# The seven level products of a gated head: taken in three groups over four banks, instead of one by one over two

## The chip, the cores and the metric

One core of one Trainium2 chip runs the whole program. The metric is the time on the device in microseconds (us), lower is better. A core has five engines that run their own instruction streams and wait for each other by semaphores: TensorE (PE in the rows, PEld for its weight loads), VectorE (DVE), ScalarE (ACT), GpSimd (POOL) and SyncE (SP), which issues the transfers.

## The reference

Two transformer blocks of two layers each, on 512 tokens of width 1024, in float32. The change touches one mixer of the second block, a gated linear recurrence over eight heads of key and value width 128:

```python
S_t = diag(f_t) S_{t-1} + k_t v_t^T ;  o_t = S_t^T q_t
scores = einsum('bhtk,bhsk,bhtsk->bhts', qc, kc, decay)   # decay = exp(b_t - b_s), b = cumsum(log f), s <= t
...
o = rmsnorm(o, norm_gain) * sigmoid(g) ;  return o @ w_o
```

The decay differs by key channel, so it can't be taken out of the product as one factor.

## The kernel before

**Levels.** Inside each block of 128 tokens the kernel halves the block again and again: `HALVES = [64, 32, 16, 8, 4, 2, 1]`. At level `lv`, each node of 2h tokens is cut into a left and a right half of h tokens, and its middle row of `b_` is the reference point. VectorE writes the differences to the middle into an operand buffer (`sub`), ScalarE takes the exponential of all 512 columns, VectorE multiplies the right halves by the queries and the left halves by the keys (`mul`), TensorE takes four products of 128 x 128 by 128 x 64, one for each token block, and VectorE puts the entries of that level into `hdiag` under a mask (`pred`, a copy_predicated). The diagonal itself comes first, from plain products of keys and queries. What lies between the four blocks comes from four wider products, the cross products, whose operands are `hx128` and `hx256` and whose results leave the banks `tp[0]` and `tp[1]` to `hoff` by ScalarE.

**Buffers.** The three operand buffers `hx[0]`, `hx[1]`, `hx[2]` are named cosT, sinT and negc in the rows; `hx128` and `hx256` are the two halves of wf_raw. Level `lv` uses `hx[lv % 3]` and the bank `sc[lv % 2]`. hdiag_t is `hdiag`, hoff_t is `hoff`.

**Slots.** Each engine's order is written out by hand. `hg_head` runs over 16 slots `k`; an engine does in slot `k` what its branches for that `k` say, in the order in which they stand in the source. In the same slots the projections of the following head are computed ("current" is the head whose scores are made, "following" the next): TensorE has 96 matmuls of 128 x 512 for it (four weight columns, eight k tiles, three terms of a split into a high and a low part), and `share` issues six in each slot, behind the slot's own products. They are the acc rows of line L633. VectorE takes the projected rows out of `acc`, prepares the next head's keys, queries and decays, and splits weights (L1168); ScalarE has the exponentials and logarithms for it.

**Order in a head.** Before, VectorE does `sub(k - 1)`, `mul(k - 2)` and `pred(k - 3)` in slot k; TensorE takes level `lv` in slot `lv + 3`; so each level's result is fetched in the slot in which its product is issued. In slot 9 VectorE normalises the head before (L1692, L1695), in slot 10 it multiplies the cross operands (L1640, L1641), and TensorE takes the cross products in slot 12 (L1054 to L1057). In slot 15 TensorE multiplies `hdiag` and `hoff` by the values (L1066, L1069), once ScalarE has copied `hoff` (L2038, L2039). TensorE runs the slot 0 products of L1035. L2007 is the exponential of a level, L1596 and L1597 are `sub`, L1602 and L1603 `mul`, L1609 `pred`, L633 the projections.

**The last head.** Head 7 has no following head; its slots share only 30 matmuls of the output projection.

Of the kernel before, what the change touches and what calls it, by code (L numbers as in the profile page):

```python
# [25 lines left out]
ACT = mybir.ActivationFunctionType  # L26
# [3 lines left out]
P = 128  # L30
# [81 lines left out]
HG_SLOTS = 16  # L112
HALVES = [64, 32, 16, 8, 4, 2, 1]


# [53 lines left out]
def two_blocks(nc, x, positions, attn_pre_g, w_in, forget_bias, lam_q1, lam_k1, lam_q2, lam_k2, diff_sub_g,  # L169
# [3 lines left out]
    with ExitStack() as ctx:  # L173
# [123 lines left out]
        aux = psum("aux")  # L297
        x_banks = [tp, sc]


# [320 lines left out]
        def _(pe):  # L621
# [395 lines left out]
            def hg_head(pp, par, current=True, following=True, previous=True, first=False, work=()):  # L1017
# [8 lines left out]
                for k in range(HG_SLOTS):  # L1026
                    if current and k == 0:
# [8 lines left out]
                        mm.then_inc(level_scored, 1)  # L1036
                    if current and 3 <= k < 3 + len(HALVES):
                        lv = k - 3
                        h = HALVES[lv]
                        x = hx[lv % 3]  # L1040
                        pe.wait_ge(level_mul, 7 * i + lv + 1)
                        if lv or not first:
                            pe.wait_ge(level_taken, 8 * i + lv)
                        for b in range(NB):
                            right = x[:, b * P:b * P + P].rearrange("p (n e j) -> p n e j", e=2, j=h)[:, :, 1]
                            mm = pe.matmul(sc[lv % 2][:, b * HD:b * HD + HD], x[:, b * P:b * P + P], right,  # L1046
                                           start=True, stop=True)
                        mm.then_inc(level_scored, 1)
                    if current and k == 12:

                        pe.wait_ge(cross_mul, i + 1)
                        if not first:
                            pe.wait_ge(cross_taken, i)
# [54 lines left out]
        def _(v):  # L1108
# [471 lines left out]
            def hg_head(pp, par, current=True, following=True, previous=True, first=False):  # L1580
# [6 lines left out]
                def sub(lv):  # L1587

                    x, b = nodes(hx[lv % 3], HALVES[lv]), nodes(b_, HALVES[lv])
                    h = HALVES[lv]  # L1590
                    mid = b[:, :, 0, h - 1:h].broadcast_to([P, S // (2 * h), h])
                    if lv == 0:
                        v.wait_ge(hg_decay_ready, i + 1)
                    if lv >= 3 or not first:
                        v.wait_ge(level_scored, 8 * i + 1 + lv - 2)
                    TT(x[:, :, 1], b[:, :, 1], mid, ALU.subtract)  # L1596
                    TT(x[:, :, 0], mid, b[:, :, 0], ALU.subtract).then_inc(level_sub, 1)  # L1597

                def mul(lv):
                    x = nodes(hx[lv % 3], HALVES[lv])  # L1600
                    v.wait_ge(level_exp, 7 * i + lv + 1)
                    TT(x[:, :, 1], x[:, :, 1], nodes(q, HALVES[lv])[:, :, 1], ALU.mult)  # L1602
                    TT(x[:, :, 0], x[:, :, 0], nodes(kk, HALVES[lv])[:, :, 0], ALU.mult).then_inc(level_mul, 1)  # L1603

                def pred(lv):
# [4 lines left out]
                                      level_mask[:, lv].rearrange("p (n j) -> p n j", j=HALVES[lv]),  # L1610
                                      sc[lv % 2][:, 0:NB * HD].rearrange("p (n j) -> p n j", j=HALVES[lv])).then_inc(level_taken, 1)

                for k in range(HG_SLOTS):
                    if current:
# [12 lines left out]
                        if 2 <= k < 9:  # L1627
                            mul(k - 2)
                        if 3 <= k < 10:
                            pred(k - 3)  # L1630
                        if k == 7:
# [86 lines left out]
        def _(a):  # L1718
# [275 lines left out]
            def hg_head(pp, par, current=True, following=True, previous=True, first=False):  # L1994
# [4 lines left out]
                for k in range(HG_SLOTS):  # L1999
                    if current:  # L2000
# [3 lines left out]
                        if 1 <= k < 8:  # L2004
                            lv = k - 1
                            a.wait_ge(level_sub, 7 * i + lv + 1)
                            ACTV(hx[lv % 3], hx[lv % 3], ACT.Exp).then_inc(level_exp, 1)  # L2007
                        if k == 11:
# [7 lines left out]
                        if k == 9:  # L2016
                            a.wait_ge(hg_decay_ready, i + 1)
                            a.wait_ge(hg_col_ready, i + 1)
                            if not first:
                                a.wait_ge(cross_scored, i)  # L2020
# [107 lines left out]
```

## Time and profile before

| | |
|---|---|
| time before, median of 3 runs | 2715.2 us (2714.83 to 2715.46) |
| the profiled execution's own time | 2711.78 us |
| its span, first to last instruction | 2710.0 us |
| TensorE busy | 2610.4 us, 96% of the span |
| VectorE busy | 1657.0 us, 61% |
| ScalarE busy | 746.8 us, 28% |
| mean granted TensorE clock | 0.984 |

The gated heads stand at about 2030 to 2308 us of the span. The chain that ended last is 81% TensorE over the whole span. A matmul's recorded duration overlaps its neighbours', so what it costs in a stream is read from one start to the next. Idle time in brackets is counted from the modelled end of the instruction before.

### The profile page before, as it was taken

The numbers are of one execution on the slowest core, as the hardware profiler recorded it, in microseconds if no ns is written. First come the engines' busy times: TensorE is split into PE (matmuls) and PEld (weight loads), VectorE is DVE, ScalarE is ACT, GpSimd is POOL, SyncE is SP. The second block draws the span as 40 slices with busy tenths as digits, with TensorE's granted clock in tenths as the row PEclk, the third lists the DMA queues.
The fourth block names the chain that finished last, engine by engine and source line by source line (L and its number), as shares of the span: only waits on it lengthen the run. The fifth ranks groups of instructions, "written<-read, shape, count | busy, mean of one in ns | idle before, by whom it ended". The sixth has DMA issues, their size and how long they took to land.

```text
span 2710.0 us, 38394 instructions
## 1 busy us (share of the span) xinstructions
PE 2610.4 (96%) x12250; PEld 2059.1 (76%) x12250; DVE 1657.0 (61%) x2625; ACT 746.8 (28%) x1391; POOL 453.5 (17%) x454
## 2 busy tenths in 40 slices
PE   8999899999899989999899989999999999999999
PEld 5776688887667668888766658888888887788887
DVE  6755666454775566645567776644458888564452
ACT  3333232120333332212145541100025555210000
POOL 4111112112111111121201101211111110111111
PEclk9999999999899999999999989999999999999999
DMA  3221233333122123333311113333332221233333
GB/s 110 55 63 54 77 88 100 93 101 101 48 55 63 55 70 101 94 99 94 92 47 55 54 32 94 100 93 101 93 93 63 63 62 47 78 93 100 94 100 94
DMA packets 417270, 214.80 MB, mean 79 GB/s; under 512 B 6819, under 2 KB 416014, under 8 KB 417166
## 3 DMA queue, kind: packets, MB, share of 16 engines
q1 hardware_dynamic: 416144, 212.89, 27.3%
q8 instruction: 59, 0.97, 0.2%
q10 hardware_dynamic: 1022, 0.58, 0.1%
q14 instruction: 45, 0.37, 0.0%
HBM read 211.34 MB, written 2.10 MB: 79 GB/s over the span
## 4 chain that ended last, share of the span: by engine, by line
PE 81%; DVE 10%; ACT 4%; issue 4%; POOL 1%; DVEq 0%; ACTq 0%; POOLq 0%
PE acc L633 69%; PE sc L740 2%; PE sc L1046 1%; DVE scratch L1438 1%; PE tp L633 1%; DVE w_lo L1168 1%; PE tp L763 1%; PE po L786 1%; PE po L633 1%; PE aux L646 1%; DVE scratch L1432 1%; ACT scratch L1914 1%; DVE xT L1357 1%; ACT scratch L1912 0%; PE tp L902 0%
## 5 line engine op out<-in xcount | busy, mean ns | idle before, releaser
L633 PE MATMUL acc<-h_hi,w_hi 128*128 128x512 f32 x1968 | 814.1, 414 | 31.0 <-DVE h_lo L1146 24.2
L576 POOL TENSOR_SCALAR w_hi<-w_raw 128x1024 fp32r<-128x1024 f32 x390 | 415.1, 1065 | 2211.6 <-PE acc L633 2134.3
L633 PE MATMUL acc<-h_hi,w_lo 128*128 128x512 f32 x1968 | 776.0, 394 | 0.0
L633 PE MATMUL acc<-h_lo,w_hi 128*128 128x512 f32 x1968 | 774.7, 394 | 0.0
L1168 DVE TENSOR_TENSOR w_lo<-w_raw,w_hi 128x1024 fp32r<-128x1024 f32 x390 | 477.4, 1224 | 75.6 <-POOL w_hi L576 75.5
L633 PEld LDWEIGHTS acc<-h_hi,w_hi 128*128 128x128 f32 x1968 | 373.2, 190 | 147.3 <-issue 46.4
L633 PE MATMUL acc<-mid_hi,w_hi 128*128 128x512 f32 x1120 | 440.4, 393 | 7.3 <-DVE mid_lo L1699 3.2
L633 PE MATMUL acc<-mid_lo,w_hi 128*128 128x512 f32 x1120 | 439.8, 393 | 0.0
L633 PE MATMUL acc<-mid_hi,w_lo 128*128 128x512 f32 x1120 | 438.6, 392 | 0.0
L633 PEld LDWEIGHTS acc<-h_hi,w_lo 128*128 128x128 f32 x1968 | 372.9, 190 | 81.4 <-issue 1.4
L633 PEld LDWEIGHTS acc<-h_lo,w_hi 128*128 128x128 f32 x1968 | 373.8, 190 | 80.0 <-issue 10.9
L633 PEld LDWEIGHTS acc<-mid_hi,w_hi 128*128 128x128 f32 x1120 | 211.3, 189 | 55.9 <-DVE w_lo L1168 4.5
L633 PEld LDWEIGHTS acc<-mid_lo,w_hi 128*128 128x128 f32 x1120 | 211.4, 189 | 44.7 <-issue 2.1
L633 PEld LDWEIGHTS acc<-mid_hi,w_lo 128*128 128x128 f32 x1120 | 211.3, 189 | 44.2 <-issue 0.8
L1511 DVE TENSOR_TENSOR xT<-xT,acc 128x512 f32 (+1 forms) x80 | 55.0, 688 | 201.8 <-PE acc L633 201.8
L1975 ACT ACTIVATE mid_hi<-scratch 128x512 f32 x64 | 40.5, 633 | 471.9 <-DVE scratch L1550 471.9
L1547 DVE TENSOR_TENSOR scratch<-acc,rstd 128x512 f32<-128x512 f32 x64 | 44.2, 691 | 130.6 <-PE acc L633 122.1
L1293 DVE CUSTOM_DVE_ANT_0 scratch<-sc,mask_row 128x128 f32<-128x128 f32 (+3 forms) x128 | 62.3, 487 | 80.3 <-PE sc L740 40.8
L1825 ACT ACTIVATE scratch<-scratch,stat 128x128 f32<-128x128 f32 (+3 forms) x128 | 72.0, 563 | 134.4 <-DVE stat L1293 134.4
L1883 ACT ACTIVATE mid_hi<-scratch 128x512 f32 x44 | 27.8, 632 | 202.9 <-DVE scratch L1398 202.9
L1736 ACT ACTIVATE scratch<-yT 128x512 f32 x32 | 20.2, 632 | 208.7 <-DVE yT L1366 137.3
L1391 DVE TENSOR_TENSOR scratch<-acc,rstd 128x512 f32<-128x512 f32 x42 | 29.0, 691 | 76.4 <-PE acc L633 76.4
(316 smaller groups left out, 2672.9 us busy)
## 6 DMA issues: line engine op xcount, KB each, us to landing
w_raw<-in_mlp_w_dram SPq DMA_DIRECT2D x128, 512.0 KB, 4.1
w_raw<-in_w_in_dram SPq DMA_DIRECT2D x48, 512.0 KB, 3.9
w_raw<-in_w_gate_dram SPq DMA_DIRECT2D x44, 512.0 KB, 3.8
w_raw<-in_w_up_dram SPq DMA_DIRECT2D x44, 512.0 KB, 3.8
w_raw<-in_w_down_dram SPq DMA_DIRECT2D x32, 512.0 KB, 4.2
w_raw<-in_hg_w_in_dram SPq DMA_DIRECT2D x32, 512.0 KB, 4.1
w_raw<-in_sb_w_qkv_dram SPq DMA_DIRECT2D x24, 512.0 KB, 3.8
w_raw<-in_w_out_dram SPq DMA_DIRECT2D x16, 512.0 KB, 4.1
```

The lines of the kernel that those rows point to most:

```text
L576: nc.gpsimd.tensor_scalar(to, w_raw[:, slot], 1.0, 1.0, ALU.mult, ALU.mult).then_inc(w_rounded, 1)
L633: mm = pe.matmul(bank[:], w[:, k], r[:, k], start=(k == 0 and i == 0), stop=(k == k_tiles - 1 and i == 2))
L646: pe.matmul(aux[:], ones[:, 0:P], pair_sum[q % 2], start=(q == 0), stop=last).then_inc(aux_done if last else square_summed, 1)
L740: mm = pe.matmul(sc[m][:, 0:n], qT[p % 2][r, t * P:t * P + P], kT[p % 2][r, 0:n], start=True, stop=(p < NDIFF))
L1168: TT(w_lo[:, slot], w_raw[:, slot], w_hi[:, slot].bitcast(F32), ALU.subtract).then_inc(w_split, 1)
L1293: v.tensor_tensor_reduce(prob[k % 4][:, 0:n], sc[k % 2][:, 0:n], mask_row[:, S - n:S], 1.0, BIG, ALU.add, ALU.min, stat[:, k % 4:k % 4 + 1 ...
L1391: TT(up, banks[1][:], rstd[:], ALU.mult).then_inc(evacuated[1], 1)
L1511: TT(dst, dst, acc[slot][:], ALU.add).then_inc(evacuated[slot], 1)
L1547: TT(gate, acc[i][:], rstd[:], ALU.mult).then_inc(evacuated[i], 1)
L1825: ACTV(prob[k % 4][:, 0:n], prob[k % 4][:, 0:n], ACT.Exp, bias=stat[:, k % 4:k % 4 + 1], scale=-1.0, accum_out=stat[:, 4 + k % 4:5 + k % 4 ...
L1883: ACTV(mid_hi[:, c % 2, ds(j, 1)], hid, ACT.Copy).then_inc(mid_hi_ready, 1)
L1975: ACTV(mid_hi[:, c % 2, ds(2 * m + i, 1)], hid, ACT.Copy).then_inc(mid_hi_ready, 1)
```

## The change

Level products are issued in three groups: levels 0 and 1 in slot 4, levels 2 and 3 in slot 6, levels 4, 5 and 6 in slot 9. The banks of the seven levels are sc[0], sc[1], tp[0], tp[1], sc[0], sc[1], tp[0], and the operand buffers hx[0], hx[1], hx[2], hx128, hx[0], hx[1], hx[2]. The masked copies go to slots 4, 5, 6, 7, 9, 9 and 10. `sub` and `mul` stay in their slots. The waits follow the buffers and banks: some on the cross products of the head before, one of TensorE's cross products on the last masked copy, one of ScalarE's cross exponentials on the level 3 product. No arithmetic is added or removed.

```diff
+LEVELS_AT = {4: (0, 1), 6: (2, 3), 9: (4, 5, 6)}
+PREDICATED_AT = {4: (0,), 5: (1,), 6: (2,), 7: (3,), 9: (4, 5), 10: (6,)}
...
+        level_x = [hx[0], hx[1], hx[2], hx128, hx[0], hx[1], hx[2]]
+        level_bank = [sc[0], sc[1], tp[0], tp[1], sc[0], sc[1], tp[0]]
...
-                    if current and 3 <= k < 3 + len(HALVES):
-                        lv = k - 3
+                    for lv in LEVELS_AT.get(k, ()) if current else ():
                         h = HALVES[lv]
-                        x = hx[lv % 3]
+                        x = level_x[lv]
                         pe.wait_ge(level_mul, 7 * i + lv + 1)
-                        if lv or not first:
-                            pe.wait_ge(level_taken, 8 * i + lv)
+                        if lv == 1:
+                            pe.wait_ge(level_taken, 8 * i + 1)
+                        if lv == 2 and not first:
+                            pe.wait_ge(cross_taken, i)
+                        if lv >= 4:
+                            pe.wait_ge(level_taken, 8 * i + 2 + lv - 4)
...
                         pe.wait_ge(cross_mul, i + 1)
+                        pe.wait_ge(level_taken, 8 * i + 8)
...
-                    if lv >= 3 or not first:
-                        v.wait_ge(level_scored, 8 * i + 1 + lv - 2)
+                    if lv == 3 and not first:
+                        v.wait_ge(cross_scored, i)
+                    if lv >= 4:
+                        v.wait_ge(level_scored, 8 * i + 2 + lv - 4)
...
-                        if 3 <= k < 10:
-                            pred(k - 3)
+                        for lv in PREDICATED_AT.get(k, ()):
+                            pred(lv)
...
                             a.wait_ge(hg_col_ready, i + 1)
+                            a.wait_ge(level_scored, 8 * i + 5)
```

TensorE in a head of the loop, around what were slots 7 to 9. Before, levels 4, 5 and 6 (L1046, operands cosT, sinT, negc by turns) each stand in front of six projection matmuls; this is level 4, six matmuls and level 5:

```order
L1046 MATMUL sc<-sinT 128x64 x4
L633 MATMUL acc<-h_hi,w_hi 128x512
L633 MATMUL acc<-h_lo,w_hi 128x512
L633 MATMUL acc<-h_hi,w_lo 128x512
L633 MATMUL acc<-h_hi,w_hi 128x512
L633 MATMUL acc<-h_lo,w_hi 128x512
L633 MATMUL acc<-h_hi,w_lo 128x512
```

In the change the three levels stand together in slot 9 (the register rows hold the values of the waits):

```order
L1053 MATMUL sc<-cosT 128x64 x4
L1044 REGISTER_ALU
L1050 REGISTER_ALU
L1053 MATMUL sc<-sinT 128x64 x4
L1044 REGISTER_ALU
L1050 REGISTER_ALU
L1053 MATMUL tp<-negc 128x64 x4
```

Level 4's product moved behind twelve projection matmuls that were behind it, level 5's behind six.

VectorE in the second head, slots 7 to 10. Before (L1609 is the masked copy of levels 4, 5 and 6):

```order
L1609 COPY_PREDICATED hdiag_t<-level_mask,sc 128x64x4
L1635 TENSOR_TENSOR hg_col<-yT 128x1
L1602 TENSOR_TENSOR cosT<-cosT,yT 128x256
L1603 TENSOR_TENSOR cosT<-cosT,yT 128x256
L1609 COPY_PREDICATED hdiag_t<-level_mask,sc 128x128x2
L1660 SCALAR_TENSOR_TENSOR scratch<-scratch 128x512
L1662 TENSOR_TENSOR scratch<-scratch 128x512
L1168 TENSOR_TENSOR w_lo<-w_raw,w_hi 128x1024
L1609 COPY_PREDICATED hdiag_t<-level_mask,sc 128x256
L1692 SCALAR_TENSOR_TENSOR scratch<-scratch,gains 128x512
```

And in the change, from the copy of the same level 4 on (L1619 is the masked copy, L1702 what was L1692, L1650 what was L1640):

```order
L1619 COPY_PREDICATED hdiag_t<-level_mask,sc 128x64x4
L1619 COPY_PREDICATED hdiag_t<-level_mask,sc 128x128x2
L1702 SCALAR_TENSOR_TENSOR scratch<-scratch,gains 128x512
L1705 TENSOR_TENSOR scratch<-scratch 128x512
L1675 TENSOR_SCALAR yT<-scratch,lower 128x512
L1619 COPY_PREDICATED hdiag_t<-level_mask,tp 128x256
L1650 TENSOR_TENSOR wf_raw<-wf_raw,yT 128x2x128
```

The copy of level 5 moved from behind the last `mul` to behind the weight split, and the copy of level 6 to right ahead of the cross operands' multiplies.

## Rows read from the trace of the kernel before

**Rows 1.** Busy by windows: us, PE, PEld, DVE, ACT, POOL; then granted clock.

```profile
2106.00:2142.00 36.00, 35.44 (x194) 29.43 (x193) 30.49 (x66) 19.06 (x37) 4.47 (x4) 1.00 0.21 59
...
2286.00:2310.00 24.00, 20.25 (x104) 16.07 (x104) 14.25 (x38) 11.07 (x24) 0.00 (x0) 0.86 0.04 13
```

**Rows 2.** TensorE's waits, 2036 to 2302 us: total, times, longest.

```profile
PE tp L1054 <- DVE wf_raw L1641: 5.7, 7, 2.6
```

**Rows 3.** Timeline of TensorE in head 2: start, us, instruction.

```profile
2112.15 1.00 PE L1046 MATMUL sc<-sinT 128*128 128x64 f32 x8
2112.96 0.48 PE L633 MATMUL acc<-h_hi,w_hi 128*128 128x512 f32 x1
2113.28 0.39 PE L633 MATMUL acc<-h_lo,w_hi 128*128 128x512 f32 x1
...
2118.76 0.40 PE L633 MATMUL acc<-h_hi,w_lo 128*128 128x512 f32 x1
2119.19 1.10 PE L1046 MATMUL sc<-sinT 128*128 128x64 f32 x8
...
2128.64 0.39 PE L633 MATMUL acc<-h_hi,w_lo 128*128 128x512 f32 x1
2129.54 0.49 PE L1054 MATMUL tp<-wf_raw 128*128 128x128 f32 x2 [0.52 <-DVE wf_raw L1641]
...
2134.84 0.39 PE L633 MATMUL acc<-h_hi,w_lo 128*128 128x512 f32 x1
2135.24 1.13 PE L1066 MATMUL po<-hdiag_t,yT 128*128 128x128 f32 x8
```

**Rows 4.** Timeline of VectorE in head 2.

```profile
2110.63 0.42 DVE L1603 TENSOR_TENSOR sinT<-sinT,yT 128x256 f32<-128x256 f32 x1
...
2113.33 0.45 DVE L1609 COPY_PREDICATED hdiag_t<-level_mask,sc 128x256 f32<-128x256 uint8 x1 [0.51 <-PE sc L1046]
...
2122.74 0.73 DVE L1609 COPY_PREDICATED hdiag_t<-level_mask,sc 128x256 f32<-128x256 uint8 x1 [0.95 <-PE sc L1046]
...
2125.77 0.73 DVE L1609 COPY_PREDICATED hdiag_t<-level_mask,sc 128x256 f32<-128x256 uint8 x1
...
2128.73 0.42 DVE L1640 TENSOR_TENSOR wf_raw<-wf_raw,yT 128x256 f32<-128x256 f32 x1
2129.07 0.42 DVE L1641 TENSOR_TENSOR wf_raw<-wf_raw,yT 128x256 f32<-128x256 f32 x1
```

**Rows 5.** Timeline of ScalarE in head 2.

```profile
2111.30 0.62 ACT L2007 ACTIVATE negc<-negc 128x512 f32<-128x512 f32 x1
...
2134.77 0.37 ACT L2039 ACTIVATE hoff_t<-tp 128x256 f32<-128x256 f32 x1
```

**Rows 6.** Timeline of TensorE in head 0.

```profile
2039.06 1.10 PE L1046 MATMUL sc<-cosT 128*128 128x64 f32 x8 [0.61 <-DVE cosT L1603]
...
2064.39 1.13 PE L1066 MATMUL po<-hdiag_t,yT 128*128 128x128 f32 x8 [0.50 <-ACT hoff_t L2039]
```

**Rows 7.** Timeline of VectorE and TensorE in the last head.

```profile
2295.20 0.74 DVE L1609 COPY_PREDICATED hdiag_t<-level_mask,sc 128x256 f32<-128x256 uint8 x1 [0.26 <-PE sc L1046]
...
2296.56 0.74 DVE L1609 COPY_PREDICATED hdiag_t<-level_mask,sc 128x256 f32<-128x256 uint8 x1 [0.62 <-PE sc L1046]
...
2299.94 0.80 PE L1054 MATMUL tp<-wf_raw 128*128 128x128 f32 x2 [2.57 <-DVE wf_raw L1641]
...
2304.37 1.90 PE L1066 MATMUL po<-hdiag_t,yT 128*128 128x128 f32 x8
...
2314.40 0.51 PE L633 MATMUL acc<-mid_hi,w_hi 128*128 128x512 f32 x1 [3.18 <-DVE mid_lo L1699]
```

**Rows 8.** Busy time by windows around the last head's cross products.

```profile
2300.00:2304.00 4.00, 4.00 (x12) 3.30 (x12) 1.18 (x2) 2.11 (x5) 0.00 (x0) 0.50 0.01 2
...
2312.00:2316.00 4.00, 1.60 (x7) 1.34 (x8) 2.56 (x5) 0.63 (x1) 0.43 (x1) 1.00 0.00 0
```

More of the change, by code:

```diff
@@ L1036, in hg_head @@
                         mm.then_inc(level_scored, 1)
-                    if current and 3 <= k < 3 + len(HALVES):
-                        lv = k - 3
+                    for lv in LEVELS_AT.get(k, ()) if current else ():
                         h = HALVES[lv]
-                        x = hx[lv % 3]
+                        x = level_x[lv]
                         pe.wait_ge(level_mul, 7 * i + lv + 1)
-                        if lv or not first:
-                            pe.wait_ge(level_taken, 8 * i + lv)
+                        if lv == 1:
[4 more added lines that the diff above has]
+                            pe.wait_ge(level_taken, 8 * i + 2 + lv - 4)
                         for b in range(NB):
                             right = x[:, b * P:b * P + P].rearrange("p (n e j) -> p n e j", e=2, j=h)[:, :, 1]
-                            mm = pe.matmul(sc[lv % 2][:, b * HD:b * HD + HD], x[:, b * P:b * P + P], right,
+                            mm = pe.matmul(level_bank[lv][:, b * HD:b * HD + HD], x[:, b * P:b * P + P], right,
                                            start=True, stop=True)
@@ L1587, in sub @@
                 def sub(lv):
-                    x, b = nodes(hx[lv % 3], HALVES[lv]), nodes(b_, HALVES[lv])
+                    x, b = nodes(level_x[lv], HALVES[lv]), nodes(b_, HALVES[lv])
                     h = HALVES[lv]
@@ L1599, in mul @@
                 def mul(lv):
-                    x = nodes(hx[lv % 3], HALVES[lv])
+                    x = nodes(level_x[lv], HALVES[lv])
                     v.wait_ge(level_exp, 7 * i + lv + 1)
@@ L1610, in pred @@
                                       level_mask[:, lv].rearrange("p (n j) -> p n j", j=HALVES[lv]),
-                                      sc[lv % 2][:, 0:NB * HD].rearrange("p (n j) -> p n j", j=HALVES[lv])).then_inc(level_taken, 1)
+                                      level_bank[lv][:, 0:NB * HD].rearrange("p (n j) -> p n j", j=HALVES[lv])).then_inc(level_taken, 1)
                 for k in range(HG_SLOTS):
@@ L2006, in hg_head @@
                             a.wait_ge(level_sub, 7 * i + lv + 1)
-                            ACTV(hx[lv % 3], hx[lv % 3], ACT.Exp).then_inc(level_exp, 1)
+                            ACTV(level_x[lv], level_x[lv], ACT.Exp).then_inc(level_exp, 1)
                         if k == 11:
```

## The prediction

> **What bounds the kernel now.** I read first the busy time by windows. In a middle head TensorE is busy 35.44 of 36 us at a full clock, VectorE 30.49, ScalarE 19.06 [rows 1]. So heads 0 to 6 are bound by TensorE, and only small holes in its stream can be won; VectorE has 5.5 us of room in 36. The last head has few projection matmuls to cover its waits: TensorE is busy 20.25 of 24 us at a mean clock of 0.86 [rows 1].
>
> Next, TensorE's waits: seven times it waits before the cross products for VectorE's multiplies, 5.7 us in all [rows 2]. The longest is the last head's 2.57 [rows 7], which leaves 3.1 us in six heads, 0.52 each.
>
> Then the timeline of TensorE in one middle head, head 2, where a hole is read from start to start. Between 2113.28 and 2118.76 stand sixteen projection matmuls and two levels, 5.48 us: with 0.23 for a matmul, a level has 0.90. That leaves three holes [rows 3]:
> - before level 4, 2118.76 to 2119.19 is 0.43, of which 0.23 is the matmul's: **0.20**;
> - before the cross products, 2128.64 to 2129.54 is 0.90: **0.67**. L1641, the last multiply of the cross operands, releases them;
> - before the value products, 2134.84 to 2135.24 is 0.40: **0.17**. ScalarE's copy of hoff ends at 2134.77 + 0.37 = 2135.14 [rows 5], just ahead of the start.
>
> Last, why VectorE is late with L1641. The last half of its second `mul` starts at 2110.63, and such an instruction takes 0.34 from start to start (2128.73 to 2129.07), so VectorE is free at 2110.97. The cross operands are done at 2129.07 + 0.34 = 2129.41. In these 18.44 us it waits twice for a level's products, 0.51 and 0.95. The copies of levels 5 and 6 also run longer, 0.73 each against 0.45 for level 1's [rows 4]; I count 0.2 more for each. About 1.9 us of the 18.44 is not work.
>
> **The change part by part.**
>
> *Work.* Nothing is added: the same products, subtractions, multiplies and masked copies.
>
> *Joining levels on TensorE.* One level is eight pairs of a weight load and a product: 0.90 us, 0.11 a pair. The first matmul behind it takes 2113.28 - 2112.96 = 0.32 instead of 0.23 [rows 3]. If this 0.09 is paid only on the way out of a group, three groups instead of seven save 4 x 0.09 = 0.35 us in a head; if it only shows that the last pair is still running, nothing. The ends are 0 and 0.35. I take 0, since the 0.90 holds the 0.09 already and is an even eight times 0.11.
>
> The Trainium skill, "TensorE: Matmul & The Clock Gate", section "LDWEIGHTS (loading the stationary operand)", prices a load by its columns at 1.2 GHz: an estimate of 107 ns for 128. By that page eight loads are 0.85 us wherever they stand and joining saves nothing; the row's 0.11 agrees.
>
> *TensorE's order.* In the change level 1 starts where it did, at 2112.15, and level 0 right ahead of it, at 2111.25. Level 6 also keeps its place behind as much work as now. Without the 0.20 hole: before, level 4 would start at 2118.99 and level 6 two slots of 0.90 + 6 x 0.23 = 2.28 later, at 2123.55. New, level 6 starts at 2123.55, level 5 at 2122.65, level 4 at 2121.75.
>
> *The level 4 hole.* Now its operands are ready at about 2119.1, just ahead of 2119.19. In the change `mul(4)` is not later and is wanted at 2121.75. **The 0.20 is gone**, with 2.6 us of cover. Level 6's operands are ready now when VectorE falls idle, 2122.74 - 0.95 = 2121.79, and wanted at 2123.55.
>
> *VectorE up to the cross operands.* It is free at 2110.97 as before. `sub(3)` takes 0.67 and ends at 2111.64. `mul(2)` then waits for ScalarE's exponential, which ends at 2111.30 + 0.62 = 2111.92 [rows 5]: a new wait of 0.3 us. Behind it stand level 0's copy and a weight split for projections two slots on. A result can be copied 2113.33 - 2112.15 = 1.18 us after its level's start [rows 3, 4]; level 0's is there at 2112.43, before VectorE comes. The copies of levels 1, 2 and 3 come a slot behind their products or with one level of work between. Level 3's buffer, hx128, was read last by the head before.
>
> The end of the last `mul`, 2121.79 now, becomes 2121.79 - 0.51 - 0.34 (level 4's copy comes later) + 0.3 = 2121.2. Then two operations for the next head's keys and a split: 2125.77 - 2122.74, less the long copy of 0.54, is 2.5 us [rows 4]. VectorE comes to slot 9's copies at 2123.7. Level 4 can be read from 2121.75 + 1.18 = 2122.93, level 5 from 2123.83, when its copy is due at 2124.0; level 6's from 2124.73, and its copy is due behind the normalising, a microsecond later. Since level 5 has only 0.2 to spare I count 0.3 for waiting there. Of the 1.9 us, 0.6 comes back: the cross operands are done 1.3 earlier, at 2128.1.
>
> *The cross products.* TensorE comes to them at 2128.64 + 0.23 - 0.20 = 2128.67. **The 0.67 is gone**, with 0.5 to spare. Their new wait for the last copy costs nothing, as that copy is ahead of the multiplies on VectorE. ScalarE's cross exponentials follow VectorE's slot 8, which is earlier too; their new wait for level 3's product is some slots old by then.
>
> *The value products.* From cross operands to value products the chain runs over VectorE's scan, ScalarE's logarithms behind it and the copies of hoff: 2135.24 - 2129.41 = 5.83 us. TensorE's own work from cross to value products is 5.70 - 0.17 = 5.53 [rows 3]. New, the chain gives 2128.1 + 5.8 = 2133.9, TensorE 2128.67 + 5.53 = 2134.2. **The 0.17 is gone**, by 0.3: the thinnest margin.
>
> Heads 1 to 6: 6 x (0.20 + 0.67 + 0.17) = 6.2 us. The end with joined levels is 8.3.
>
> *Head 0.* Before level 0 stands a bracket of 0.61, before the value products one of 0.50 [rows 6]. In head 2 a bracket of 0.52 was a hole of 0.67 [rows 3], so these are 0.76 and 0.65. The first is covered by six matmuls in the new slot 4, the second goes as above: 1.4 us.
>
> *Head 7.* VectorE is the chain up to the cross operands. It waits 0.26 and 0.62 for levels 5 and 6, with two long copies [rows 7]: 1.3 us. In the change TensorE still starts each level as soon as its own `mul` is done, and behind level 6's `mul` VectorE has two copies and the normalising before it needs the result. **1.3 us**.
>
> *The clock.* After 2.57 us without a matmul the clock is 0.50, TensorE's 1.2 GHz level [rows 7, 8]. From L1054 to L1066 it takes 4.43 us with four matmuls between; head 2's 5.53 with eighteen gives 5.53 - 14 x 0.23 = 2.31 at a full clock [rows 3, 7], a loss of 2.1. L1066 itself is 1.90 against 1.13: 0.8 more. Together 2.9 us. In the change the hole is 1.3 shorter, and I take it that the clock stays up. Against that, a hole of 3.18 us before 2314.40 left the clock at 1.00 [rows 7, 8], so length isn't all that counts, and this hole, which moves by some 12 us, may fall badly instead: from 0 to as much as the 2.9 just priced. I take -1.5.
>
> The Trainium skill, same page, section "Why this matters for your kernels", asks for no idle gap over about 3 us. The trace doesn't bear it out as a limit: 2.57 us brought the clock down and 3.18 did not.
>
> **Sum:** 6.2 + 1.4 + 1.3 + 2.9 - 1.5 = 10.3 us. Against the profiled execution's 2711.8 that is 2701.5; the timed runs lie 3.4 above it, which I take as a constant: **2704.9 us**.
>
> **The rivals.**
> 1. *Holes go, the clock falls as before.* 8.9 us: 2706.3; with the later hole falling too, 2707.8. For it: nothing shows when the clock is judged.
> 2. *The wait moves to slot 9.* Levels 5 and 6 are read behind a group of three. If their copies wait 0.9 more than I count, one level's work, the cross operands are late by 0.4 and the hoff chain by 0.6, so 0.6 of each head's 1.04 stays: 6 x 0.4 + 1.4 + 1.3 = 5.1, and with half of the clock's 2.9 6.5: 2708.7.
> 3. *Nothing in it.* If new waits take all of VectorE's 1.9 us, only the 0.20 and head 0's 0.76 are won: 2 us, 2713.2. It needs 1.3 us of waiting in slots 4 to 10 that I don't see.
> 4. *Slower.* If a level's result can be copied only when its whole group has ended, level 4's copy waits until 2123.55 + 1.18 = 2124.7, 1.0 us behind VectorE's arrival. That alone leaves the cross operands at 2129.1, still not slower; it decides from 1.3 us on. With 2.5 us (the group's result a whole share late), 7 x 1.2 - 2 = 6.4 slower: 2721.6. Against it: every level's last product has its own increment.
> 5. *Joining saves too.* 7 x 0.35 on top: 2702.4, and 2700.9 without the -1.5.
>
> **How the numbers follow.** My forecast 0.38, rival 1 0.20, rival 2 0.17, rival 3 0.07, rival 4 0.05, rival 5 0.13. The range leaves out rivals 4 and 3 and a piece of rival 2 above, and ends at rival 5 below: 2701 to 2711. About 0.2%, 5.4 us, is what a measurement can tell from no change, so faster means under 2709.8. Faster is 0.38 + 0.20 + 0.13 and most of rival 2, 0.10: 0.81. The same 0.14, slower 0.05.
>
> **What the changed profile would show.** TensorE's waits for wf_raw fall from 5.7 us in seven times to one in the last head, under 2 us; no middle head waits before level 4 or before the value products, and each is 1.0 us shorter; VectorE waits at the masked copies at most once a head, briefly, in slot 9; the clock around the last head's cross products is 1.00. I'm wrong if the cross products of middle heads still wait for VectorE, if the value products wait over 0.3 us for hoff, or if a copy in slot 9 waits 0.9 us.

## The result, and the profile after

The changed kernel takes **2721.8 us** (median of ten runs, 2718.4 to 2727.0) against 2714.7 us before (ten runs beside them, 2712.0 to 2715.8): a ratio of 1.0031, with an interval of 1.0023 to 1.0040. It is slower by about 7 us. The prediction, 2704.9 us in a range of 2701 to 2711, is wrong in its sign.

The profiled execution took 2726.96 us (span 2725.2), the slowest of the ten and 15.2 us more than the 2711.78 before; it had the lowest mean granted clock, 0.977 against 0.978 to 0.984. So what follows shows where the loss lies, and shows the clock's part larger than in the median. I measure a head from the first product L1039 (before: L1035) of one to that of the next. The seven heads 0 to 6 took 247.8 us in the profile before and 260.05 us in this one.

Busy time by windows of the changed kernel (the columns of [rows 1]): two middle heads' worth, two microseconds of head 2 behind its cross products, and the last head from its first product to its value products.

```profile
2106.00:2142.00 36.00, 33.90 (x181) 28.82 (x180) 31.13 (x64) 17.80 (x36) 3.78 (x4) 0.95 0.18 50
2142.00:2178.00 36.00, 33.89 (x191) 28.88 (x189) 31.70 (x64) 18.89 (x37) 4.23 (x4) 1.00 0.19 54
...
2133.00:2135.00 2.00, 2.00 (x8) 1.73 (x7) 1.97 (x6) 0.12 (x1) 0.00 (x0) 0.50 0.00 0
...
2293.00:2320.00 27.00, 24.69 (x100) 20.74 (x99) 19.09 (x47) 12.19 (x26) 1.05 (x1) 0.62 0.07 21
```

TensorE is busy 33.9 of 36 us where it was 35.44 [rows 1]: there is more standing, not less. And the granted clock is 0.95 in the first row, where it was 1.00: part of that stretch, the third row, ran at 0.50.

TensorE's waits, from 2030 to 2325 us: total, times, longest.

```profile
PE tp L1062 <- DVE wf_raw L1651: 12.8, 7, 2.1
PE sc L1053 <- DVE cosT L1613: 1.2, 1, 1.2
PE po L1074 <- ACT hoff_t L2050: 0.6, 1, 0.6
```

The wait that was to vanish, that of the cross products for VectorE's multiplies, has grown from 5.7 us in seven times [rows 2] to 12.8; the last head's is 0.57 of it, the six others 1.9 to 2.1 each. The waits before level 4 and before the value products are gone from the middle heads, as forecast.

Timeline of TensorE in two middle heads, head 2 and head 3: the last projection matmul, the cross products (L1062 on) and the value products (L1074).

```profile
2129.93 0.39 PE L637 MATMUL acc<-h_hi,w_lo 128*128 128x512 f32 x1
...
2132.42 0.77 PE L1062 MATMUL tp<-wf_raw 128*128 128x128 f32 x2 [2.10 <-DVE wf_raw L1651]
2132.98 0.64 PE L1063 MATMUL tp<-wf_raw 128*128 128x128 f32 x2
...
2139.53 1.05 PE L1074 MATMUL po<-hdiag_t,yT 128*128 128x128 f32 x8
...
2170.32 0.46 PE L1062 MATMUL tp<-wf_raw 128*128 128x128 f32 x2 [2.11 <-DVE wf_raw L1651]
2170.61 0.39 PE L1063 MATMUL tp<-wf_raw 128*128 128x128 f32 x2
...
2175.82 1.06 PE L1074 MATMUL po<-hdiag_t,yT 128*128 128x128 f32 x8
```

The hole is 2132.42 - 2129.93 - 0.23 = 2.26 us; it was 0.67. Both heads have it. But in head 2 the rows behind it are long (L1063 0.64 us against 0.39): the clock has fallen to its 1.2 GHz level, and from L1062 to L1074 it takes 7.11 us; in head 3 the clock stayed up and it takes 5.50. So a head is 36.29 us long in head 3 and 37.8 to 37.9 in the five others of heads 1 to 6 (35.4 before). The cost has two parts, then: **0.9 us a head at a full clock, the cross products' hole being 1.6 longer and the other holes gone, and 1.6 us wherever the clock falls behind it**. With head 0, which is 0.87 shorter, that is 6 x 0.9 + 5 x 1.6 - 0.9 = 12.5 us, and the rows show 12.2. The other 3 us of this execution's 15 lie in the last head: it takes 26.9 us from its first product to its value products, at a mean clock of 0.62, where it took 23.84 at 0.89 before. Its clock fell ahead of its cross products, 1.3 us behind a stop of 1.2 us before level 0. I can't put this down to the change: among the thirteen profiled executions of this document, one for each kernel, the stretch is shortest, 21.1 us at 1.00, in experiment 1 and longest, 28.35 us at 0.60, in experiment 2, which has the order of before. Every total contains it.

Why are the cross operands late? Timeline of GpSimd and VectorE in head 2 of the changed kernel: the rounding of the weights (L580, L576 before), and beside each the instruction of VectorE that is longer than its kind.

```profile
2113.30 1.04 POOL L580 TENSOR_SCALAR w_hi<-w_raw 128x1024 fp32r<-128x1024 f32 x1 [6.67 <-PE acc L637]
2113.67 0.95 DVE L1612 TENSOR_TENSOR negc<-negc,yT 128x256 f32<-128x256 f32 x1 [0.23 <-ACT negc L2017]
...
2122.38 1.05 POOL L580 TENSOR_SCALAR w_hi<-w_raw 128x1024 fp32r<-128x1024 f32 x1 [8.04 <-PE acc L637]
2122.41 1.02 DVE L1645 TENSOR_TENSOR hg_col<-yT 128x1 f32<-128x1 f32 x1
...
2130.26 0.41 DVE L1651 TENSOR_TENSOR wf_raw<-wf_raw,yT 128x256 f32<-128x256 f32 x1
2130.52 1.05 POOL L580 TENSOR_SCALAR w_hi<-w_raw 128x1024 fp32r<-128x1024 f32 x1 [7.08 <-PE acc L637]
2130.59 1.25 DVE L1650 TENSOR_TENSOR wf_raw<-wf_raw,yT 128x256 f32<-128x256 f32 x1
2131.76 0.41 DVE L1651 TENSOR_TENSOR wf_raw<-wf_raw,yT 128x256 f32<-128x256 f32 x1
```

Read the ends. The rounding of 2122.38 ends at 2123.43, and so does L1645, the addition of two columns, which takes 0.15 us elsewhere. The rounding of 2130.52 ends at 2131.57; L1650 ends 0.27 later. L1612 ends 0.28 behind its rounding too. An instruction of VectorE with two operands in SBUF that starts under a rounding of GpSimd stands until the rounding is over; the rows of heads 1 to 6 are alike in this. The three cost 0.54 + 0.87 + 0.83 = 2.2 us of VectorE's time in a head, all of it ahead of the cross operands.

Before, the same roundings cost little. They are released by the end of a projection unit, so they lie at fixed places of TensorE's order, and VectorE happened to stand there. Timeline of the kernel before, head 2 again:

```profile
2112.51 1.22 POOL L576 TENSOR_SCALAR w_hi<-w_raw 128x1024 fp32r<-128x1024 f32 x1 [7.58 <-PE acc L633]
...
2121.92 1.04 POOL L576 TENSOR_SCALAR w_hi<-w_raw 128x1024 fp32r<-128x1024 f32 x1 [8.20 <-PE acc L633]
...
2129.22 1.17 POOL L576 TENSOR_SCALAR w_hi<-w_raw 128x1024 fp32r<-128x1024 f32 x1 [6.25 <-PE acc L633]
2129.40 0.69 DVE L1668 TENSOR_TENSOR scratch<-acc,rstd 128x512 f32<-128x512 f32 x1
2130.00 0.93 DVE L1670 TENSOR_TENSOR scratch<-scratch 128x512 f32<-128x512 f32 x1
```

VectorE's two waits for level products, 0.51 us up to 2113.33 and 0.95 us up to 2122.74 [rows 4], lie, but for 0.13 us, under the first two roundings (2112.51 to 2113.73, 2121.92 to 2122.96). The third came when the last of the cross operands was under way already; behind it L1670 took 0.93 us instead of 0.68. **The waits that the change removes were the cover of the roundings.**

The Trainium skill, "SBUF — State Buffer", section "Who interferes with whom", states this: VectorE's second SBUF input comes through a read port that it shares with GpSimd, it contends with a GpSimd instruction that reads SBUF and not with one that only writes, and the lock is exclusive. The rows agree: 0.42 becomes 0.95 and 1.25, 0.15 becomes 1.02, while VectorE's multiply of acc (in PSUM) by rstd, L1668 of the last rows, starts under a rounding and takes its usual 0.69 us. The experiments below test the rest.

### The profile page after: what moved, and what is told of

Read it like the earlier page. It is cut to its first block and busy times, and to the rows that moved or that the text cites. A ratio compares the mean times of both kernels' runs of the same rounds, so it can differ in the third digit from the quotient of the medians.

```text
span 2725.2 us, 38387 instructions
## 1 busy us (share of the span) xinstructions
PE 2622.1 (96%) x12250; PEld 2076.1 (76%) x12250; DVE 1669.6 (61%) x2625; ACT 746.2 (27%) x1391; POOL 450.7 (17%) x454
## 5 line engine op out<-in xcount | busy, mean ns | idle before, releaser
L580 POOL TENSOR_SCALAR w_hi<-w_raw 128x1024 fp32r<-128x1024 f32 x390 | 413.0, 1059 | 2228.6 <-PE acc L637 2153.1
L637 PEld LDWEIGHTS acc<-h_lo,w_hi 128*128 128x128 f32 x1968 | 375.4, 191 | 82.4 <-issue 12.5
(324 smaller groups left out, 2704.0 us busy)
```

The source lines that it names most:

```text
L580: nc.gpsimd.tensor_scalar(to, w_raw[:, slot], 1.0, 1.0, ALU.mult, ALU.mult).then_inc(w_rounded, 1)
L637: mm = pe.matmul(bank[:], w[:, k], r[:, k], start=(k == 0 and i == 0), stop=(k == k_tiles - 1 and i == 2))
```

## The experiments

Theory A: the roundings hold VectorE's instructions up, the cross products' wait grows by that, and the longer stop of TensorE lets its clock fall. Each kernel was run beside the kernel before (2713.1, 2713.4 and 2714.0 us in the three groups, experiments 1 to 4, 5 to 8 and 9 to 11, 17 to 27 runs each). The change itself was run beside one of 2714.7, so across groups I compare ratios and not times.

### 1. The change, with GpSimd's rounding replaced by a fill

In the units of the gated heads GpSimd writes 1.0 instead of rounding. It reads nothing. The low part is then the weight less 1, so the two parts still sum to the weight, but coarsely. Of the edit, the instruction alone:

```diff
-nc.gpsimd.tensor_scalar(to, w_raw[:, slot], 1.0, 1.0, ALU.mult, ALU.mult).then_inc(w_rounded, 1)
+nc.gpsimd.memset(w_hi[:, slot].bitcast(F32), 1.0).then_inc(w_rounded, 1)
```

> The change, but in the units of the gated heads GpSimd writes w_hi with the constant 1.0 instead of rounding w_raw into it, so it reads nothing from SBUF; the projections' values there are not those of the reference. Theory A (GpSimd's rounding holds a read path that VectorE needs for a second SBUF operand; the new order puts three roundings a head on VectorE's two-operand instructions, 0.54 + 0.87 + 0.83 us): the three long instructions at L1612, L1645 and L1650 fall to 0.42, 0.15 and 0.42, TensorE no longer waits 2 us before the cross products, a middle head takes 34.4 us instead of 36.3 to 37.9, the stage clock is 1.00 in heads 1 to 6, and the time is 2703 to 2707 us. Rival B (the instructions are long because of the new buffers and banks: wf_raw shared with ScalarE, tp with TensorE): they stay long, and the time stays at 2718 to 2727.

Measured: **2699.2 us** (2698.6 to 2701.5), ratio 0.9950, interval 0.9936 to 0.9964. The groups of VectorE's instructions over the heads, with busy time and mean ns of one:

```profile
L1662 DVE TENSOR_TENSOR wf_raw<-wf_raw,yT 128x256 f32<-128x256 f32 x14 | 6.1, 437 | 0.0
L1624 DVE TENSOR_TENSOR negc<-negc,yT 128x256 f32<-128x256 f32 x14 | 5.9, 419 | 1.4 <-ACT negc L2029 1.4
...
L1657 DVE TENSOR_TENSOR hg_col<-yT 128x1 f32<-128x1 f32 x7 | 1.0, 149 | 0.0
```

None is long: a fill of 0.95 us that only writes holds nobody up. The cross products wait in the last head alone, the clock is 1.00 from 2030 to 2280 us, and a middle head takes 34.07 us. With the rounding's reads replaced by a fill, the ratio falls from 1.0031 to 0.9950, about 22 us, and the change is faster than before.

### 2. The kernel before, with the same fill

> The kernel before with the same constant fill in place of GpSimd's rounding in the gated heads. Theory A: before, two of the four roundings of a head fell where VectorE stood waiting for a level's product, so only L1670 was longer (0.93 instead of 0.68); taking the reads away wins about 0.2 us a head, 1 to 3 us in all: 2712 to 2714. Rival B: no difference at all, within 1 us of before. Rival C (GpSimd's rounding costs VectorE the same in both orders): 5 us or more faster.

Measured: 2712.2 us, ratio 0.9993 (0.9984 to 1.0002). The total can't tell theory A from rival B, which allowed 1 us; it rules out rival C. The heads can: they are 35.1 us instead of 35.4. So the fill by itself is worth 0.3 us a head; what it undoes in the changed kernel is a meeting that the change has brought about.

### 3. The change's banks and buffers, but one level a slot

```diff
-LEVELS_AT = {4: (0, 1), 6: (2, 3), 9: (4, 5, 6)}
-PREDICATED_AT = {4: (0,), 5: (1,), 6: (2,), 7: (3,), 9: (4, 5), 10: (6,)}
+LEVELS_AT = {3: (0,), 4: (1,), 5: (2,), 6: (3,), 7: (4,), 8: (5,), 9: (6,)}
+PREDICATED_AT = {4: (0,), 5: (1,), 6: (2,), 7: (3,), 8: (4,), 9: (5,), 10: (6,)}
```

> The change's four banks and four buffers, but the levels one by one in slots 3 to 9 as before, each copied one slot later (4 to 10). Joining is gone, the wait of VectorE for a product stays removed. Theory A: what matters is that VectorE no longer stands still when GpSimd rounds; so the long instructions appear here as well, one to three a head, the cross products wait over 1 us, and the time is within 3 us of the change (2717 to 2725). Rival D (the groups themselves are what costs: TensorE in bursts, results later): no long instructions, a head of 34.4 to 34.6 us, 2705 to 2708.

Measured: 2713.0 us, ratio 0.9996 (0.9987 to 1.0005): neither theory's number. VectorE's groups over the heads:

```profile
L1176 DVE TENSOR_TENSOR w_lo<-w_raw,w_hi 128x1024 fp32r<-128x1024 f32 x28 | 34.1, 1216 | 4.3 <-POOL w_hi L580 4.3
...
L1670 DVE SCALAR_TENSOR_TENSOR scratch<-scratch 128x512 f32<-128x512 f32 x7 | 10.0, 1425 | 0.0
L1680 DVE TENSOR_TENSOR scratch<-scratch 128x512 f32<-128x512 f32 x7 | 6.2, 888 | 0.0
```

The roundings met other instructions: L1670, 1.43 us instead of 0.7, and L1680, 0.89 instead of 0.7; and once a head VectorE came to a weight split before GpSimd had rounded, a wait of 0.6 us. The cross products wait 0.79 us, the clock stays at 1.00 and a head takes 35.51. All four roundings are there and read as much, so it isn't their reading as such that costs. I had expected the meetings at the same places; which instruction is hit depends on a few tenths.

### 4. The change, with eight matmuls more ahead of the cross products

To tell the clock's part from the hole's, TensorE does 2 us of useless work (128x512, into po, which the value products start afresh) where it would stand.

```diff
+if not first:
+    pe.wait_ge(hg_o_taken, i)
+for _ in range(8):
+    pe.matmul(po[:], h_hi[:, 0, 0:P], h_hi[:, 0], start=True, stop=True)
 pe.wait_ge(cross_mul, i + 1)
```

> The change with eight matmuls of 128 x 512 (about 1.8 us) into the idle po bank just ahead of the cross products' wait; their results are overwritten. Theory A2 (besides the wait of 2.3 us, the clock falls to its 1.2 GHz level behind it in five heads of six and costs 1.6 us each): the wait before the cross products shrinks to about 0.4 us, the clock stays at 1.00 in heads 1 to 6, every head takes 36.3 us, and the time falls by 5 to 9 us against the change, to 2713 to 2717, though work was added. Rival E (the clock costs nothing beyond the wait): the same time as the change or up to 1 us slower.

Measured: 2714.5 us (2711.1 to 2720.1), ratio 1.0009 (1.0000 to 1.0018). Timeline of TensorE in one of its heads:

```profile
2127.04 1.98 PE L1061 MATMUL po<-h_hi 128*128 128x512 f32 x8
2129.31 0.46 PE L1066 MATMUL tp<-wf_raw 128*128 128x128 f32 x2 [0.30 <-DVE wf_raw L1655]
```

The cross products start when they would have, a head takes 36.3 us, and the clock is 1.00 in heads 1 to 6. **Adding work made the kernel faster**, from a ratio of 1.0031 to 1.0009, about 6 us: that is the clock's part of the loss in the median.

### 5. The change, with the roundings on ScalarE

The weights are rounded as ever, by another engine. ScalarE is busy 19 of 36 us and rounds the 32 units of the gated heads at four places of its order where it mostly stood. GpSimd's part of the edit, which skips these units, is left out here.

```diff
+def act_round(half, slot):
+    a.wait_ge(w_landed[slot], 16 * half + 16)
+    a.wait_ge(unit_done, 2 * half + slot + 1)
+    a.wait_ge(w_rounded, 2 * half + slot)
+    ACTV(w_hi[:, slot], w_raw[:, slot], ACT.Copy).then_inc(w_rounded, 1)
...
+if current and k == 0: act_round(half + 2, 1)
...
+if following and k in (4, 7): act_round(half + 3, 0 if k == 4 else 1)
...
+if following and k == 11: act_round(half + 4, 0)
```

> The change, with the 32 roundings of the gated heads' weights (128x1024 each) moved from GpSimd to ScalarE; the same values are computed. Theory A (VectorE's instructions with two inputs in SBUF are held up while GpSimd's rounding reads and writes there; the rounding's reading is what matters): no instruction of VectorE of 0.42 us becomes one of 0.95 or 1.25 us, the cross products wait less than 0.3 us, the clock stays at full speed in heads 1 to 6, a middle head takes 34.1 to 34.6 us (ScalarE has about 1.1 us four times a head to find, and some of it may delay an exponential), 2698 to 2705 us in all. Rival E (the fill of the first experiment was fast because its constant weights changed what TensorE and its clock do, not because GpSimd stopped reading): here the weights are the real ones, so heads of over 36 us and 2712 to 2722 us. Rival F (any second engine that reads SBUF holds VectorE up): instructions of 0.95 to 1.25 us stay, now beside ScalarE's roundings, and the time is 2710 us or more.

Measured: **2704.7 us** (2703.3 to 2705.3), ratio 0.9966, interval 0.9954 to 0.9978. Windows over a middle head, then from its timeline a weight split of VectorE (L1179), a rounding of ScalarE with the addition of two columns under it, and the cross products:

```profile
2102.00:2138.00 36.00, 35.57 (x202) 30.47 (x201) 30.33 (x66) 24.17 (x43) 0.00 (x0) 1.00 0.25 71
```

```profile
2111.99 1.23 DVE L1179 TENSOR_TENSOR w_lo<-w_raw,w_hi 128x1024 fp32r<-128x1024 f32 x1 [0.35 <-ACT w_hi L2011]
...
2119.08 1.06 ACT L2011 ACTIVATE w_hi<-w_raw 128x1024 fp32r<-128x1024 f32 x1
2119.22 0.15 DVE L1648 TENSOR_TENSOR hg_col<-yT 128x1 f32<-128x1 f32 x1
...
2127.61 0.46 PE L1065 MATMUL tp<-wf_raw 128*128 128x128 f32 x2 [0.43 <-DVE wf_raw L1654]
```

ScalarE works 5 us more, GpSimd nothing, and VectorE's 128x256 products are back at 0.42 us. A head is 34.6 us long. That rules out rival E, since the weights are the real ones, and rival F, since ScalarE reads the same 128x1024 and holds nobody up: the addition under its rounding takes 0.15 us. The cross wait of 0.43 us is a little over what I allowed; VectorE stands 0.35 us before the weight split of 2111.99 until ScalarE has rounded, where experiment 1 has no such wait. This version beats both kernels.

### 6 and 7. One rounding taken away, or the two others

The third rounding of a head (2130.5 us) is replaced by the fill in one kernel, the first two (2113.3 and 2122.4) in the other.

```diff
+for n in range(4):
+    half, slot = U_HG // 2 + 2 * i + n // 2, n % 2
+    if n in (0,):        # experiment 6; experiment 7 has (2, 3)
+        other_unit(half, slot)
+    else:
+        round_unit(half, slot, w_hi[:, slot], 2 * half + slot + 1)
```

> The change, with only one of the four roundings of a head (the one that ran at 2130.5 us, under the products that make the cross operands) replaced by a fill with 1.0; its low part is then the weight less 1. Theory A: wf_raw's 1.25 us instruction goes back to 0.42, the two others (0.95 at negc, 1.02 at hg_col) stay. The cross products' wait shrinks from 2.1 us to about 1.3 us, and if it is this wait that brings the clock down, the clock stays up and a head takes 36.29 - 0.83 = 35.5 us: 2721.8 - 6 x 2.3 = 2708 us (2705 to 2712). If the clock falls through the groups themselves and not through the wait, heads take about 37 us: 2716 to 2718 us.

> The change, with the two roundings that ran at 2113.3 and 2122.4 us replaced by fills with 1.0, the third left. Theory A: 0.95 at negc and 1.02 at hg_col become 0.42 and 0.15, wf_raw's 1.25 us stays. The cross products then wait about 0.9 us, the clock stays up, and a head takes 36.29 - 1.41 = 34.9 us: 2721.8 - 6 x 2.9 = 2704.5 us (2702 to 2708). Clock falling through the groups themselves: 2713 us or more.

Measured, third alone: 2712.4 us, ratio 0.9995 (0.9986 to 1.0004). A head is 35.4 to 35.5 us as expected, and the clock stays up in the middle heads behind a shorter stop:

```profile
2128.32 0.46 PE L1076 MATMUL tp<-wf_raw 128*128 128x128 f32 x2 [1.29 <-DVE wf_raw L1665]
```

Head 6, whose third rounding is still one, kept a stop of 1.90 us and took 36.3. The total is a little above its range of 2705 to 2712. The last head ran at the lower level:

```profile
2290.00:2300.00 10.00, 10.00 (x43) 9.52 (x43) 6.44 (x19) 3.44 (x10) 0.00 (x0) 0.50 0.00 0
```

But so it did in the profile of the changed kernel, so this doesn't explain the total, and what does isn't shown.

Measured, the two others: 2705.4 us, ratio 0.9968 (0.9956 to 0.9981), in its range, but one step is not as I said: I expected the cross products to wait 0.9 us, and in the middle heads they don't wait. The third rounding no longer meets the cross operands. It meets the scan, the multiply ahead of which is L1694:

```profile
2123.88 0.68 DVE L1694 TENSOR_TENSOR scratch<-scratch 128x512 f32<-128x512 f32 x1
2124.59 2.09 DVE L1698 TENSOR_TENSOR_SCAN yT<-ones,scratch 128x128 f32<-128x128 f32 x4
```

```profile
2123.94 1.52 POOL L580 TENSOR_SCALAR w_hi<-w_raw 128x1024 fp32r<-128x1024 f32 x1 [7.21 <-PE acc L651]
```

The multiply was there first, kept its 0.68 us, and GpSimd's rounding took 1.52 us instead of 1.05; the scan behind it then took 2.09 instead of 1.37. Whoever comes second pays. The copies of hoff behind the scan came late, and the value products waited 0.5 us in each head.

### 8. The third rounding kept, but later

GpSimd waits for the cross operands before it rounds; what it reads is the same.

```diff
+if n == 0:
+    pool.wait_ge(cross_mul, i - 1)
+round_unit(half, slot, w_hi[:, slot], 2 * half + slot + 1)
```

> The change, with the third rounding kept on GpSimd with all its reading, but held back until the cross operands are done (GpSimd waits for VectorE's last product of them), so about 0.5 to 1 us later; the same values are computed. Theory A: wf_raw's 1.25 us instruction is 0.42 again and the delay falls on the multiplication of acc by rstd or the one behind it, which TensorE doesn't wait for: cross wait 1.3 us, a head 35.5 us, 2708 us (2704 to 2712). Theory G (what costs is how much GpSimd reads in a head, wherever it stands, since every 1.05 us of it holds VectorE up by as much): the head's length stays at 36.3 us or more, 2713 to 2722 us.

Measured: 2713.1 us, ratio 0.9999 (0.9990 to 1.0008). Timelines of a head, GpSimd, VectorE, ScalarE, TensorE:

```profile
2131.90 1.05 POOL L580 TENSOR_SCALAR w_hi<-w_raw 128x1024 fp32r<-128x1024 f32 x1 [8.28 <-DVE wf_raw L1658]
```

```profile
2132.04 1.45 DVE L1687 TENSOR_TENSOR scratch<-scratch 128x512 f32<-128x512 f32 x1
```

```profile
2137.33 0.38 ACT L2057 ACTIVATE hoff_t<-tp 128x256 f32<-128x256 f32 x1
```

```profile
2131.76 0.46 PE L1069 MATMUL tp<-wf_raw 128*128 128x128 f32 x2 [1.25 <-DVE wf_raw L1658]
...
2137.96 1.13 PE L1081 MATMUL po<-hdiag_t,yT 128*128 128x128 f32 x8 [0.53 <-ACT hoff_t L2057]
```

The cross products' wait is 1.25 us, as expected. But the rounding now holds up L1687, 1.45 instead of 0.68 us; the scan is late by as much, ScalarE's logarithms behind the scan too, and the copies of hoff stand behind those in ScalarE's order. TensorE waits 0.53 us before the value products instead. A head takes 36.2 us, hardly less than the 36.3 of the change at a full clock. So theory A had the hit right and the place where it hurts too small: what I called off the path is the hoff chain of the prediction. The time lies above theory A's range and at the edge of theory G's; what speaks against G is experiment 3 and the kernel before, with the same roundings and heads of 35.5 and 35.4 us. Against the changed kernel it is still about 8 us faster, with the same length of a full-clock head: two shorter stops in place of one long one, and the clock stays at 1.00 in heads 0 to 6.

### 9. The kernel before, with the roundings on ScalarE

> The kernel before, with the 32 roundings moved to ScalarE as in the experiment that did so to the change. Theory A: before has only one instruction of VectorE under a rounding (0.93 instead of 0.68 us), and two of the roundings ran while VectorE stood waiting, so little is to be had: heads of 35.0 to 35.3 us (the fill gave 35.1), 2710 to 2714 us. If it is the moved rounding itself that makes the faster version fast, and not its meeting with the groups, the gain is the same as there, about 9 us: 2704 us.

Measured: 2712.8 us, ratio 0.9994 (0.9985 to 1.0003), heads of 35.2 us: moving the roundings helps the kernel before by nothing that can be told. Only with the change do they matter, and with them out of the way the change is worth the step from 0.9994 to 0.9966, about 7.6 us.

### 10. Roundings on ScalarE, the groups undone

Experiment 5 with the two tables of experiment 3.

> The roundings on ScalarE and the change's banks and buffers, but level products again one by one in slots 3 to 9, each with its copy in the next slot. Theory A: with no collision left the kernel has no TensorE wait on level products either (each product's bank and operands are ready a slot ahead), and the prediction found joining worth about nothing: heads of 34.4 to 34.9 us, 2701 to 2708 us. If the groups themselves carry the gain (fewer stops of TensorE between the projections), heads stay at 35.2 us or more: 2710 us or more.

Measured: 2705.8 us (2704.0 to 2707.6), ratio 0.9969 (0.9958 to 0.9981), the same as with the groups. Over a middle head TensorE hardly stands any more:

```profile
2102.00:2138.00 36.00, 35.99 (x200) 30.43 (x199) 29.61 (x65) 24.27 (x44) 0.00 (x0) 1.00 0.23 65
```

A head takes 34.3 us, even less than the 34.6 with groups. Against experiment 9, which differs by the banks, the fourth buffer and the copies a slot later, it is 7.0 us faster; so these three together make the gain (no run takes them apart), and the groups themselves give nothing.

### 11. Roundings on ScalarE, and TensorE made to stand

```diff
 pe.wait_ge(level_taken, 8 * i + 8)
+if following:
+    pe.wait_ge(hg_decay_ready, i + 2)
```

> The version with roundings on ScalarE (2704.7 us, heads of 34.6 us, cross wait 0.43 us), with one wait added: the cross products wait until VectorE's scan for the next head is done, about 2.6 us after the cross operands. TensorE then stands about 3.0 us in slot 12 of each of heads 0 to 6, with no collision on VectorE. If it is the standing of TensorE that brings the clock down, as theory A says of the changed kernel, rows behind the cross products show half speed, the granted clock of the heads is under 0.98, and a head takes 37.2 us plus about 1.6: 2704.7 + 7 x 2.6 + 6 x 1.6 = 2732 us (2726 to 2738). If the clock doesn't follow from the length of this stop, it stays at 1.00 in the heads and the time is 2704.7 + 7 x 2.6 = 2723 us (2719 to 2726).

Measured: 2733.5 us (2731.5 to 2734.7), ratio 1.0071 (1.0058 to 1.0085). Windows over two heads, and the cross products of four:

```profile
2102.00:2138.00 36.00, 35.68 (x186) 29.95 (x185) 26.14 (x57) 20.26 (x38) 0.00 (x0) 0.94 0.21 60
2138.00:2174.00 36.00, 33.57 (x181) 28.88 (x182) 26.96 (x58) 20.41 (x38) 0.00 (x0) 0.95 0.18 49
```

```profile
2100.69 0.77 PE L1067 MATMUL tp<-wf_raw 128*128 128x128 f32 x2 [2.96 <-DVE yT L1689]
...
2140.43 0.62 PE L1067 MATMUL tp<-wf_raw 128*128 128x128 f32 x2 [2.75 <-DVE yT L1689]
...
2179.07 0.49 PE L1067 MATMUL tp<-wf_raw 128*128 128x128 f32 x2 [2.76 <-DVE yT L1689]
...
2216.05 0.79 PE L1067 MATMUL tp<-wf_raw 128*128 128x128 f32 x2 [2.75 <-DVE yT L1689]
```

With no collision anywhere, a stop of 2.8 us brings the clock down by itself, but not each time: heads 1 to 6, from 2072.6 on, take 39.9, 38.6, 37.0, 38.5, 37.0 and 40.0 us, and the 0.49 of the third row is a cross product at full speed. Head 0 waited 1.94 us, and its clock fell too.

## Why the prediction was wrong

**The step that failed** is "The end of the last `mul`, 2121.79 now, becomes 2121.79 - 0.51 - 0.34 ... + 0.3 = 2121.2", and with it "the cross operands are done 1.3 earlier, at 2128.1". Both move VectorE's instructions and let each keep the length it had in the trace. The runs showed 0.95, 1.02 and 1.25 us for three that are 0.42, 0.15 and 0.42 by kind, where they fell under a rounding. I took VectorE's waits of 0.51 and 0.95 us for time that could be had. They were time in which GpSimd rounded. With them gone VectorE's operand products run under the roundings, 2.2 us are added, and the cross operands are done at 2132.1 in a head that began at 2105.23, 26.9 us in; before it was 2129.41 - 2103.53, 25.9 us. GpSimd's 4.47 us in the window of [rows 1] stood in the table that I read first, and I never asked what ran beside it. It was no rival of mine: rival 4 has the right sign, but by a group's late result, and nothing of that is in the trace.

The sum without the roundings came out nearly right, but partly by luck. In experiment 1 the cross operands are done 24.6 us into the head, 1.3 earlier than before, as I had it. Yet I had counted 0.4 us for the long copies of levels 5 and 6 as no work, and they stay long (0.75 and 0.73 us at 2127.05 and 2129.36 in the change, 0.73 in experiments 1 and 10); against that stand 0.3 us of waiting for slot 9's copies that never came, and a wait for ScalarE of 0.23 instead of 0.3.

Point by point:
- *Level 4's hole, 0.20:* gone. *Value products' hole, 0.17:* gone in the middle heads, and as thin as I called it: 0.5 us of lateness on the hoff chain shows at once in experiments 7 and 8.
- *Cross products' hole, 0.67 to be gone:* it became 2.26, by the failed step. In experiment 1, where nothing is hit ahead of them, it is gone.
- *ScalarE's new wait ahead of `mul(2)`, 0.3:* measured 0.23. *Slot 9's copies:* they don't wait, so rival 2 fell.
- *Joining saves nothing:* right; experiment 10 has the same time without any group. Rival 5 fell.
- *Head 0, 1.4 us:* measured 0.87 (35.34 to 34.47); its wait before the value products stayed, 0.6 us, the one row of that kind above. *The last head, 1.3 us:* somewhat too large. In the changed kernel its clock hides it. In experiments 1 and 5 its cross products start 18.4 us behind its first product, against 2299.94 - 2280.53 = 19.4 before: 1.0 us. Their own wait shrinks by 0.3 alone, 2.25 and 2.23 against 2.57 [rows 7], since TensorE comes to them earlier too.
- *The clock:* I priced it for the last head and for the hole behind it alone, and never for a middle head. It fell in five of six of those, 1.6 us each. That is a second failed term, and it hangs on the first: it stood at nothing, since I had the wait there gone.
- *Size of the holes:* with nothing hit, a head fell from 35.4 to 34.07 us in experiment 1, 1.3 where I had 1.04. I had counted the stops and not what stands behind one. In head 2 before, level 4's products take 0.91 us from start to start behind their hole (2119.19 to 2120.10), the other levels 0.81 to 0.83; the value products L1066 take 0.96, and 0.93 in experiment 1. That is half of the 0.26; I have not traced the rest.

That the predicted 2704.9 us and the 2704.7 of experiment 5 agree is chance. I had forecast a gain of 10.3 us from 2715.2; experiment 5 is 8.7 faster than the 2713.4 run beside it. In the profiles its heads 0 to 6 are 6.9 us shorter than before, where I had 7.6.

What stays open: why the clock fell behind one stop and not behind the next of the same length, and so how much of the last head's scatter is in each total.

## What to carry to other kernels

A wait seen on one engine may be the place where another engine uses what they share; before counting it as won, lay that engine's timeline beside it and see which instructions would come to stand there. Here it takes one look: do GpSimd's reads of SBUF overlap VectorE's instructions with two SBUF inputs, before, and where would they overlap after. And when a wait of TensorE may grow, price the clock with it: a hole that grew by 1.6 us cost 1.6 us more in the heads where the clock fell.

## What the runs showed of the hardware

- A collision of VectorE with GpSimd costs by the other's length, not one's own: an addition of 128x1 took 1.02 us instead of 0.15 under a rounding of 1.05 us. The one that came second paid, GpSimd too (1.52 instead of 1.05 us in experiment 7).
- A fill of 128x1024 by GpSimd (0.95 us, no read) and a copy of as much by ScalarE (1.04 to 1.06 us) lengthened none of VectorE's 128x256 products.
- Stops of TensorE of 1.1 to 1.3 us before the cross products left its clock at 1.00 in all eleven middle heads of experiments 6 and 8. Stops of 1.9 to 2.1 us brought it to 0.50 in five of six heads of the changed kernel and in head 0 of experiment 11, and not in head 6 of experiment 6; stops of 2.75 to 2.96 us in four of six (experiment 11); the 3.2 us before the output projection in 5 of 13 profiled executions. Eight useless matmuls in the gap made the changed kernel about 6 us faster.
